# Last down projection: three of its four pairs of output tiles take 16 of 22 row blocks by Strassen's scheme

## The reference

```python
        h2 = rmsnorm(x, g_ffn[l])
        x = x + (jax.nn.silu(h2 @ w_ff_gate[l]) * (h2 @ w_ff_up[l])) @ w_ff_down[l]
    return rmsnorm(x, g_final)
```

## Time and profile before

| what | value |
|---|---|
| median of 3 runs | 1532.28 us (1531.96 to 1532.83) |
| the profiled execution | 1532.8 us |
| its span, first to last instruction | 1531.0 us |
| TensorE busy | 1505.6 us, 98% |
| VectorE, ScalarE, GpSimd busy | 941.7, 560.1, 1006.7 us |

### The profile page before, as it was taken

One profiled execution on the slowest core, in us unless ns is written; L12 is line 12 of the kernel. 1 busy time (PEld: TensorE's weight loads), 2 busy tenths in 40 slices (PEclk: granted clock), 3 DMA queues, 4 the chain that ended last, 5 costly groups with the idle time before them and its releaser, 6 DMA issues.

```text
span 1531.0 us, 25810 instructions
## 1 busy us (share of the span) xinstructions
PE 1505.6 (98%) x8968; PEld 1342.5 (88%) x8968; DVE 941.7 (62%) x1424; ACT 560.1 (37%) x998; POOL 1006.7 (66%) x795
## 2 busy tenths in 40 slices
PE   7999999999999999999999999999999999999997
PEld 6998999998887899988888888888888999999886
DVE  7877787863428477787254665556467788774013
ACT  6543566640113455612032122222335565552001
POOL 4735877766666777766566576576467777776664
PEclk9999999999999999999999999999999999999999
DMA  9942333344333333433323232232232343333231
GB/s 369 403 154 74 103 100 96 110 156 155 99 106 90 96 98 111 123 89 88 98 70 95 73 92 82 80 96 82 68 97 83 100 120 97 107 98 110 96 98 55
DMA packets 218142, 172.81 MB, mean 113 GB/s; under 512 B 5216, under 2 KB 191968, under 8 KB 218080
## 3 DMA queue, kind: packets, MB, share of 16 engines
q1 hardware_dynamic: 218080, 171.98, 35.9%
HBM read 169.86 MB, written 2.10 MB: 112 GB/s over the span
## 4 chain that ended last, share of the span: by engine, by line
PE 62%; issue 2%; POOL 2%; DVE 2%; ACT 0%; DMA 0%; POOLq 0%; DVEq 0%; ACTq 0%
PE ps L923 20%; PE ps L926 20%; PE ps L927 20%; POOL tmp L817 1%; POOL w_lo L835 0%; POOL tmp L826 0%; DMA raw<-in_w_ff_up 0%; POOL rope_r L835 0%; PE ps L1355 0%; POOL w_lo L803 0%; ACT wide_hi L1420 0%; POOL w_hi L801 0%; DVE ps L2262 0%; DVE ps L2247 0%; DVE tmp L2244 0%
## 5 line engine op out<-in xcount | busy, mean ns | idle before, releaser
L803 POOL TENSOR_TENSOR w_lo<-raw,w_hi 128x1024 fp32r<-128x1024 f32 x144 | 358.2, 2487 | 12.0
L923 PE MATMUL ps<-act_hi,w_hi 128*128 128x256 f32 (+1 forms) x888 | 300.5, 338 | 2.9 <-ACT gates L1664 1.3
L926 PE MATMUL ps<-act_hi,w_lo 128*128 128x256 f32 (+1 forms) x888 | 297.2, 335 | 0.0
L927 PE MATMUL ps<-act_lo,w_hi 128*128 128x256 f32 (+1 forms) x888 | 297.0, 334 | 0.0
L923 PE MATMUL ps<-wide_hi,w_hi 128*128 128x512 f32 (+2 forms) x736 | 271.7, 369 | 1.0 <-POOL w_lo L803 0.6
L926 PE MATMUL ps<-wide_hi,w_lo 128*128 128x512 f32 (+2 forms) x736 | 271.1, 368 | 0.0
L927 PE MATMUL ps<-wide_lo,w_hi 128*128 128x512 f32 (+2 forms) x736 | 271.0, 368 | 0.0
L800 POOL TENSOR_TENSOR w_hi<-raw,zero 128x1 fp32r<-128x1 f32 x144 | 36.0, 250 | 319.5 <-PE ps L923 318.4
L923 PEld LDWEIGHTS ps<-act_hi,w_hi 128*128 128x128 f32 x888 | 169.3, 191 | 23.2 <-issue 3.2
L926 PEld LDWEIGHTS ps<-act_hi,w_lo 128*128 128x128 f32 x888 | 169.4, 191 | 17.7 <-issue 1.4
L927 PEld LDWEIGHTS ps<-act_lo,w_hi 128*128 128x128 f32 x888 | 169.4, 191 | 16.7
(11 more groups left out here) (282 smaller groups left out, 3476.5 us busy)
## 6 DMA issues: line engine op xcount, KB each, us to landing
raw<-in_w_in SPq DMA_DIRECT2D x88, 512.0 KB, 3.9
gates<-in_w_mod_t SPq DMA_DIRECT2D x20, 1024.0 KB, 10.6
raw<-in_w_ffn_up SPq DMA_DIRECT2D x40, 512.0 KB, 3.8
raw<-in_w_ffn_down SPq DMA_DIRECT2D x22, 512.0 KB, 3.3
raw<-in_w_ff_gate SPq DMA_DIRECT2D x22, 512.0 KB, 3.8
raw<-in_w_ff_up SPq DMA_DIRECT2D x22, 512.0 KB, 3.8
raw<-in_w_ff_down SPq DMA_DIRECT2D x22, 512.0 KB, 3.4
raw<-in_w_r_out SPq DMA_DIRECT2D x16, 512.0 KB, 3.5
```

Source lines behind the costliest of these rows:

```text
L803: nc.gpsimd.tensor_tensor(w_lo[:, two, :], raw[:, slot, :], f32(w_hi[:, two, :]), SUB).then_inc(split_done, 1)
L923: ins = mm(o, w, a, start=start, stop=False)
L926: mm(o, wl, a, start=False, stop=False)
L927: return mm(o, w, al, start=False, stop=stop)
```

## The change

The last down projection is now made of four pairs of output tiles (2j, 2j+1), and of twelve units of work. Pair 0 takes all 22 row blocks by plain products (units 0, 1, 2). Pairs 1 to 3 take row blocks 16 to 21 by plain products (units 3, 8, 11) and row blocks 0 to 15 by Strassen's scheme in two units of seven forms each (units 4 to 7, 9, 10); plain and Strassen parts of pairs 1 and 2 are summed in the same banks, those of pair 3 on DVE. The token sums of rows 0 to 15 (eight row pairs, k = 0 to 7) are made while pair 0 is multiplied and somewhat beyond. A panel is one output tile by eight or six row blocks. Unit 11 goes by token halves and ends the stage. The first block's down projection is left as it was.

The constants, and TensorE, the new order:

```diff
-START = [EIGHT, 0, 0]
+START = [EIGHT, 0, 0, 0, 0]
...
+T_ORDER = [("lo", 0), ("lo", 1), ("lo", 2), ("late", 0), ("lo", 3), ("late", 1), ("lo", 4), ("late", 2), ("lo", 5), ("late", 3),
+           ("lo", 6), ("late", 4), ("lo", 7), ("late", 5), ("late", 6), ("late", 7)]
+DOWN_T_BANK = (0, 6, 2, 0, 6, 0, 4, 4)
+DOWN_T_AFTER = (None, None, None, 0, 1, 3, None, 6)
...
+            def std_tile(f, u, s, out, tokens=slice(0, T), start=True, stop=True, again=False, between=None,
+                         halved=False):
+
+                j, k0, n = STD_UNITS[u]
+                p = std_panel(f, u, s)
+                pe.wait_ge(split_done, p + 1)
...
+            def strassen_unit(f, p):
+
+                j, c = p[1] + 1, p[2]
+                last_up = pair_of(f, FT - 1)
+                for form in PRODUCTS["later"]:
+                    if form in LO_POOL["later"]:
+                        pe.wait_ge(form_lo_pool, counted(LO_POOL, p, form))
+                    else:
+                        pe.wait_ge(form_lo_dve, counted(LO_DVE, p, form))
...
+                    for k in range(QUAD):
+                        if j == 1 and form in (F6, F7, F4):
+                            pe.wait_ge(t_ready, t_at(f, "lo", c * QUAD + k))
+                        elif j == 1 and form == F5:
+                            pe.wait_ge(t_ready, t_at(f, "late", c * QUAD + k))
...
+                pe.wait_ge(t_ready, t_at(f, "lo", 2))
+                for s in range(PAIR):
+                    std_tile(f, 3, s, ps[:, 2 + s, :], stop=False).then_inc(part_done, 1)
+                for n in range(4):
+                    strassen_unit(f, pair_of(3 + f, n))
+                for s in range(PAIR):
+                    std_tile(f, 8, s, ps[:, 4 + s, :], start=False, halved=s == 1).then_inc(part_done, 1)
+                for n in range(4, 6):
+                    strassen_unit(f, pair_of(3 + f, n))
+
+            def down_end():
+
+                f = 1
+                pe.wait_ge(dn_free[f], 6)
+                for s in range(PAIR):
+                    std_tile(f, 11, s, ps[:, 4 + s, halves[0]], halves[0]).then_inc(dn_done[f], 1)
+                pe.wait_ge(joined, down_joined(f, 3, "x"))
+
+                def first_sums():
+                    pe.wait_ge(dn_free[f], 10)
+                    pe.wait_ge(squares_added[3], 7)
+                    token_sums(0, [(0, 8, True)]).then_inc(norm_summed[3], 1)
+
+                std_tile(f, 11, 0, ps[:, 6, halves[1]], halves[1], again=True).then_inc(dn_done[f], 1)
+                std_tile(f, 11, 1, ps[:, 7, halves[1]], halves[1], again=True, between=(1, first_sums)).then_inc(dn_done[f], 1)
```

ACT, the copies for a row pair, and POOL, the split of a panel of a plain unit and the end of its list:

```diff
+            def down_copies(f, k):
+
+                bank, (a, b) = DOWN_T_BANK[k], down_rows(k)
...
+                if DOWN_T_AFTER[k] is not None:
+                    act.wait_ge(t_ready, t_at(f, "lo", DOWN_T_AFTER[k]))
+                if bank == 4:
+                    act.wait_ge(dn_free[f], 2)
+                do(ps[:, bank, :], f32(wide_hi[:, a, :]), ACT.Identity)
+                do(ps[:, bank + 1, halves[1]], f32(wide_hi[:, b, halves[1]]), ACT.Identity).then_inc(gained, 1)
...
+            def std_split(f, u, s):
+
+                p, slot, n = std_panel(f, u, s), unit_slot(f, u) + s, STD_UNITS[u][2] * P
+                pool.wait_ge(raw_loaded[slot], unit_loads(f, u))
+                pool.wait_ge(panel_used, p - 1)
...
+                forms(5)
+                pool.wait_ge(product_done, counted(PRODUCTS, unit[5], F6))
+                std_split(f, 11, 0)
+                std_split(f, 11, 1)
```

DVE, the token sums of one row pair and part of the list they stand in (`down_lo` and `down_late` make the lo parts, `lo` that of a form):

```diff
+            def down_parts(f, k):
...
+                tt(down_t1(k), b12, f32(wide_lo[:, a, halves[1]]), ADD)
+                tt(b11, b11, f32(wide_lo[:, a, halves[0]]), ADD)
+                link(tt(b22, b22, f32(wide_lo[:, b, halves[1]]), ADD))
+
+            def down_t_sums(f, k):
...
+                link(tt(t3, t1, b22, SUB))
+                link(tt(t1, t1, b11, SUB))
+                link(tt(b22, b22, t1, SUB))
+                link(tt(t4, f32(wide_hi[:, b, halves[0]]), b22, SUB))
+                tt(t4, t4, f32(wide_lo[:, b, halves[0]]), ADD).then_inc(t_summed, 1)
...
+            def down_late(f, k):
+
+                dve.wait_ge(t_hi_made, LOADED + t_at(f, "late", k))
+                hi, lo = (w[:, down_rows(k)[0], halves[1]] for w in (wide_hi, wide_lo))
+                tt(lo, down_t1(k), f32(hi), SUB).then_inc(t_ready, 1)
...
+                for k in range(1, 6):
+                    down_parts(f, k)
+                    down_t_sums(f, k)
+                    down_lo(f, k - 1)
+                    if k >= 3:
+                        down_late(f, k - 3)
+                for m in range(2):
+                    dve.wait_ge(dn_done[f], m + 1)
+                    residual(m)
+                down_lo(f, 5)
+                down_late(f, 3)
+                dve.wait_ge(t_ready, t_at(f, "lo", 5))
+                add6(unit[0])
+                down_parts(f, 6)
+                down_t_sums(f, 6)
+                lo(F6, 0)
+                down_lo(f, 6)
+                down_late(f, 4)
+                lo(F5, 0)
+                add3(unit[0])
+                down_parts(f, 7)
+                lo(F3, 0)
+                down_t_sums(f, 7)
```

More of the change, by code:

```diff
@@ L1205, in spread @@
                     ins.then_inc(norm_summed[3], 1)
[L1207 to L1220, removed]
-                        ins = product(ps[:, QUAD * i + o, t_], *w_block((p0 + last) % 2, c * QUAD + o),
-                                      wide_hi[:, k, t_], wide_lo[:, k, t_], i == 1 and last == 0 and c == 0, last == 1 and c == 1,
-                                      opens=i == 0 and o == 0 and c == 0)
-                    if last:
-                        ins.then_inc(dn_done[1], 1)
-                    if (i, last, o) == (1, 1, 1):
-                        pe.wait_ge(dn_free[1], KT)
-                        pe.wait_ge(squares_added[3], KT - 1)
-                        token_sums(0, [(0, KT, True)]).then_inc(norm_summed[3], 1)
-                pe.wait_ge(squares_added[3], KT - 1 + 2)
-                token_sums(1, [(0, KT + 2, False), (3, KT + 3, False)])
@@ new lines, in std_tile @@
+            def std_tile(f, u, s, out, tokens=slice(0, T), start=True, stop=True, again=False, between=None,
[3 more added lines that the diff above has]
+                pe.wait_ge(split_done, p + 1)
+                for b in range(n):
+                    if j == 0:
+                        pe.wait_ge(wide_ready[f], k0 + b + 1)
+                    for i, t_ in enumerate(halves if halved and b == 0 else [tokens]):
+                        o = out[:, t_] if halved and b == 0 else out
+                        ins = product(o, *w_block(s, b), wide_hi[:, k0 + b, t_], wide_lo[:, k0 + b, t_],
+                                      start and b == 0, stop and b == n - 1, opens=b == 0 and i == 0 and not again)
+                    if between and b == between[0]:
+                        between[1]()
+                return ins
@@ L1599, in sum_copy @@
                     act.wait_ge(t_ready, T_MADE[2] + 2 * QUAD)
+                elif begins(p) and p[0] >= 3:
+                    act.wait_ge(t_ready, t_at(p[0] - 3, "lo", 5))
                 elif begins(p):
@@ L1919, in last_square @@
                     act.wait_ge(squares_added[3], n - 2)
[L1920 to L1931 removed]
+                do(tmp[:, 0 if n == 0 else 1 if n % 2 else 4, tokens], res[:, m, tokens], ACT.Square).then_inc(res_squared[3], 1)
@@ new lines, in square_row @@
+            def square_row(m):
+                act.wait_ge(dn_free[1], m + 1)
+                if m == 0:
+                    act.wait_ge(t_ready, t_at(1, "late", 7))
+                last_square(m, m, slice(0, T))
+            down_act(1, square_row)
+            act.wait_ge(product_done, counted(PRODUCTS, pair_of(4, 4), F4))
+            for i in range(2):
+                out_gain(OUT_POOL, i)
+            for m in (6, 7):
+                act.wait_ge(dn_free[1], m + 3)
+                last_square(m, m, halves[0])
@@ L1934, in _ @@
             token_std(1)
-            for m in range(OUT_POOL, KT):
+            for m in (6, 7):
                 out_gain(m, 1)
@@ L2695, in last_added @@
                     dve.wait_ge(squares_added[3], n)
[L2697 to L2708 removed]
+            down_dve(1, down_residual, last_added)
```

387 lines of the change are left out of this document (345 added, 42 removed).

## The result

The changed kernel's median is 1535.15 us over 15 runs (1533.69 to 1535.8), against 1532.30 over 15 runs before on the same chip (1531.86 to 1533.16): a ratio of 1.0017, 95% interval 1.0009 to 1.0025. The profiled execution took 1533.96 us with a span of 1532.2, against 1532.8 and 1531.0 before.

A forecast was written before the change was run, and what follows sets the result against it. TensorE, busy for 98% of the span, was taken to bound the kernel. Columns -4.92, waits +4.2, last split +1.2 and tail -0.15 gave +0.3 on the median of 1532.28: 1532.6 us, range 1530.2 to 1535.2.

The forecast's parts named there:

- Columns, 4.92: TensorE's down-stage products fall from 120.32 to 115.40 us, saving 4.92 us.
- The waits, 4.2: TensorE waits at units 4 and 5: F6 0.2, F7 1.0, F4 2.7, F1 0.3 us late, together 4.2 us.
- DVE against POOL: DVE's T1 lo parts, reading two SBUF tensors, are blocked by POOL's instructions; waits rise from 2.5 to 4.2 us.
- the prediction's own case: T1 for k = 2 passes, several later T1 parts are blocked: 1532.6 us, range 1531.6 to 1534.3, chance 0.50.
- the rival in which all are blocked: Blocked T1 lo parts decide, k = 2's among them: waits 7.0 + 1.2, sum +3.1, 1535.4 us; chance 0.14.
- the rival in which all pass: T1's lo parts pass between POOL's instructions: waits 2.5 + 1.2, sum -1.4, 1530.9 us; chance 0.27.
- Later units, 0: Strassen units behind the first ones cost TensorE no wait, 0 us; a miss would cost about 0.5.
- The last split, 1.2: TensorE waits 1.2 us (0.9 to 1.4) for POOL's split of unit 11's second panel.
- Tail, -0.15: Behind the last product, TensorE's 0.18 us wait for a square shrinks, giving about 0.15 us.
- Sum: On the span, -4.92 + 4.2 + 1.2 - 0.15 = +0.3 us, giving a median of 1532.6.
- The rival in which the chain of sums is hidden: TensorE waits only for unit 11's split: -4.92 + 1.2 - 0.15 = -3.9, 1528.4 us, faster; chance 0.09.

The follow-up runs named there:

- the last version: Changed kernel with ACT's and DVE's lists reordered and unit 11's second panel split into the tiles of F5 and F2: 1527.18 us against 1532.65 (0.9964).
- The run with F6 first: Changed kernel with F6's lo part of unit 5 moved ahead of T1's for k = 5 to 7 on DVE: 1533.15 us against 1532.53.

## Why the prediction was right, and where it was wrong

The median lies 0.05 us inside the range and 2.55 us above the value. The mechanism was right: TensorE's columns are saved, and waits for work that DVE, ACT and POOL have not finished take the saving back. That the time still fell inside the range is partly luck, since an error in one term paid for part of one in another. Step by step:

- **Columns, 4.92.** Right: the last version, with no wait in units 3 to 11, saves 4.71. Of the other 0.2, a short gap ahead of F6 of unit 4 makes 0.17.
- **The waits, 4.2.** Wrong in the places, and by starts 5.47 in sum. F6 of unit 4 lost 0.19 (0.2 foreseen), F7 1.27 (1.0), F1 of unit 5 0.25 (0.3). F4 lost 1.47 against 2.7: T1's lo part for k = 4, which was to be held by F7's on POOL, began 0.05 us ahead of it and passed. F6 of unit 5 lost 2.29 where the prediction had nothing. This is the step that failed: the lists were followed as far as F1 of unit 5, with a price of 1.1 on some of the T1 parts for k = 5 to 7, but not through the one instruction that stands behind all three on DVE. The run with F6 first shows that it was their place that made this wait. What F4 lost less than foreseen paid for half of what F6 of unit 5 lost; that is luck.
- **What a wait costs.** The prediction counted a wait from when TensorE would begin to when its operand is ready. The next start behind the stalled matmul comes 0.10 late as well, which it left out: 0.3 over the three waits of units 4 and 5.
- **DVE against POOL.** Right: of the eight T1 parts, the five that were issued while a POOL instruction ran took 0.63 to 1.52 us and the three others 0.41, and one column was held for up to 1.25. The Trainium skill (SBUF — State Buffer, Who interferes with whom) says that a VectorE instruction with two SBUF inputs contends with a GpSimd one that reads SBUF, and that the order of issue decides which of them is blocked; the rows at 1438.28 and 1438.33, where POOL's came second and took 1.49, agree with the second half of that too. T1 of k = 2 came ahead of unit 3's second subtraction, as the prediction's own case had it, so the rival in which all are blocked did not happen; the rival in which all pass did not either. One row behind the price was misread, without effect on it: the row of 2.88 us is one of the seven executions counted in the earlier trace rows, not an eighth.
- **Later units, 0.** Right in the changed kernel, but only because TensorE reached them late, which the prediction did not say. With F6's wait gone, F1 of unit 6 waited 1.09 for the joins.
- **The last split, 1.2.** Right: 1.12 listed, 1.39 by starts.
- **Tail, -0.15.** Behind the last product the span ends 11.9 us later, against 12.4 before: -0.5, and 11.9 in the traces of all the variants too. The engines' last instruction ends no sooner behind the last product than before (8.1 us, before 7.5), so the gain lies behind the output's multiplications; its cause stays open. The first down product comes 0.25 earlier than before, which lies within what the traces here differ by.
- **Sum.** +1.95 in the down stage, -0.5 and -0.25 around it: +1.2 in the span, where +0.3 was forecast. The median rose by 2.85: most executions lie about 1 us above the three of the changed kernel that were traced. The half clock behind a wait, 1.5 us in one trace, is a cause of the right size; that it is the cause stays open.

The rival in which the chain of sums is hidden, 1528.4, was the better account of what the change can do. It needs no less work, only the order of the lists: 1528.51 was measured.

## What to carry to other kernels

Work that is moved to idle engines has to be followed through each engine's list to the first instruction that the busy engine waits for, and through the second unit as well as the first: an instruction that nobody needs yet costs what stands behind it. A list's order is worth trying before its work is cut; an engine that idles in front of a late input (ACT's 2.65 and 3.25 us here), while a later instruction of its list has its own input ready, is the place to begin. A wait removed in a chain came back at the next place in two of the runs here, so such edits are to be judged together.

## What was not expected of the hardware

TensorE's granted clock fell from 1.00 to 0.52 (mean of 3.5 us, at 1.2 GHz for nearly all of it) behind a single wait of 2.07 us in one trace, which cost 1.5 us more, and stayed at 1.00 behind waits of 2.03, 2.03, 2.02 and of 2.08 and 2.02 in four others. The start that follows a stalled matmul came 0.22 us behind it instead of 0.12. And a DVE instruction of one column with both inputs in SBUF took up to 1.25 us beside POOL, against 0.15 alone.
